# Three of the four up products of each MLP by a seven-product block scheme

## The reference

```python
def sq_relu_mlp(h, w_up, w_down):
    u = jnp.einsum('btd,df->btf', h, w_up)
    return jnp.einsum('btf,fd->btd', jnp.square(jax.nn.relu(u)), w_down)

h = h + sq_relu_mlp(rms_norm_2(h, mlp_norm_g[layer]), mlp_w_up[layer], mlp_w_down[layer])
```

## Time and profile before

| what | value |
|---|---|
| median of 3 runs | 1849.39 us (1848.42 to 1850.87) |
| the profiled execution | 1848.76 us |
| its span in the trace | 1847.0 us |
| TensorE busy (matmuls) | 1804.7 us, 98% |
| weight loads busy | 1441.0 us, 78% |
| VectorE busy | 981.4 us, 53% |
| ScalarE busy | 797.4 us, 43% |
| GpSimd busy | 476.5 us, 26% |
| DMA | 149.10 MB, 81 GB/s |

### The profile page before, as it was taken

How to read it: one execution, slowest core, us unless ns; L and a number is a source line. 1 busy time by engine, 2 the same in 40 slices (tenths; PEclk the granted TensorE clock), 3 DMA queues, 4 the chain that set the end, 5 groups by cost and what they waited for, 6 DMA issues and landing times.

```text
span 1847.0 us, 24633 instructions
## 1 busy us (share of the span) xinstructions
PE 1804.7 (98%) x9664; PEld 1441.0 (78%) x9668; DVE 981.4 (53%) x1581; ACT 797.4 (43%) x1401; POOL 476.5 (26%) x475
## 2 busy tenths in 40 slices
PE   7999999999999999999999999999999999999997
PEld 6987777776678766677888888888888788888886
DVE  5355556575546688854433434365677653333333
ACT  5236665455435365564441423233445543232412
POOL 0035551101312145560120201005677112010200
PEclk9999999999999999999999999999999999999999
DMA  5221111231012311012222222222222122222222
GB/s 182 93 71 54 48 46 60 82 97 48 23 57 96 124 65 34 30 36 70 91 102 103 92 92 102 103 91 81 81 86 75 57 92 100 96 97 97 95 98 79
DMA packets 44514, 149.10 MB, mean 81 GB/s; under 512 B 6000, under 2 KB 6384, under 8 KB 44400
## 3 DMA queue, kind: packets, MB, share of 16 engines
q1 hardware_dynamic: 44400, 147.53, 23.6%
HBM read 139.64 MB, written 2.10 MB: 77 GB/s over the span
## 4 chain that ended last, share of the span: by engine, by line
PE 87%; DVE 5%; POOL 3%; ACT 3%; issue 2%; DMA 1%; POOLq 0%; SPq 0%; DVEq 0%; ACTq 0%
PE BANK L288 23%; PE BANK L290 22%; PE BANK L289 22%; PE BANK L920 3%; PE BANK L654 2%; PE BANK L1704 1%; PE BANK L1685 1%; PE BANK L1661 1%; PE BANK L977 1%; PE BANK L2499 1%; PE BANK L639 1%; PE BANK L2474 1%; DVE LH L763 1%; POOL LH L885 1%; PE BANK L2462 1%
## 5 line engine op out<-in xcount | busy, mean ns | idle before, releaser
L256 ACT ACTIVATE WH<-WRAW 128x1024 fp32r<-128x1024 f32 x262 | 273.3, 1045 | 452.0 <-PE BANK L290 425.6
L265 DVE TENSOR_TENSOR WL<-WRAW,WH 128x1024 fp32r<-128x1024 f32 (+1 forms) x249 | 326.6, 1312 | 253.1 <-ACT WH L256 252.2
L288 PE MATMUL BANK<-HH,WH 128*128 128x512 f32 x1048 | 422.4, 403 | 11.1 <-DVE WL L265 9.6
L290 PE MATMUL BANK<-HL,WH 128*128 128x512 f32 x1048 | 409.4, 391 | 0.0
L289 PE MATMUL BANK<-HH,WL 128*128 128x512 f32 x1048 | 408.9, 390 | 0.0
L288 PEld LDWEIGHTS BANK<-HH,WH 128*128 128x128 f32 x1048 | 197.4, 188 | 60.5 <-issue 20.6
L290 PEld LDWEIGHTS BANK<-HL,WH 128*128 128x128 f32 x1048 | 197.1, 188 | 42.0
L289 PEld LDWEIGHTS BANK<-HH,WL 128*128 128x128 f32 x1048 | 197.6, 189 | 40.4 <-issue 2.9
L2339 POOL TENSOR_TENSOR HID<-TMP,HID 128x512 fp32r<-128x512 f32 x64 | 82.8, 1293 | 527.1 <-ACT HID L2320 527.1
L288 PE MATMUL BANK<-HID,WH 128*128 128x512 f32 (+1 forms) x520 | 200.8, 386 | 0.0
L290 PE MATMUL BANK<-HID,WH 128*128 128x512 f32 (+1 forms) x520 | 200.6, 386 | 0.0
(11 more groups left out here) (413 smaller groups left out, 3113.6 us busy)
## 6 DMA issues: line engine op xcount, KB each, us to landing
WRAW<-in_w SPq DMA_DIRECT2D x77, 512.0 KB, 3.4
WRAW<-in_wu SPq DMA_DIRECT2D x64, 512.0 KB, 3.2
WRAW<-in_wd SPq DMA_DIRECT2D x64, 512.0 KB, 3.2
WRAW<-in_w0o SPq DMA_DIRECT2D x8, 512.0 KB, 3.5
WRAW<-in_w1o SPq DMA_DIRECT2D x8, 512.0 KB, 3.4
WRAW<-in_wc SPq DMA_DIRECT2D x8, 512.0 KB, 3.2
WRAW<-in_w2o SPq DMA_DIRECT2D x8, 512.0 KB, 3.2
WRAW<-in_w3o SPq DMA_DIRECT2D x8, 512.0 KB, 3.2
```

Of the source, the lines that this page charges most:

```text
L256: e.activation(WH[b % NS][:, 0:n], WRAW[b % NR][:, 0:n], ACT.Copy).then_inc(*inc("s_high", ("high", b)))
L265: e.tensor_tensor(WL[b % NS][:, 0:n], WRAW[b % NR][:, 0:n], WH[b % NS][:, 0:n].bitcast(F32), ALU.subtract).then_inc(*inc("s_low_pool" if p ...
L288: e.matmul(dst, ah, bh, start=first and i == 0, stop=False)
L290: made = e.matmul(dst, ah, bl, start=False, stop=last and i == len(sets) - 1)
```

## The change

Chunk 0 of each MLP keeps its tiles. For chunks 1, 2 and 3 the up product is computed by Strassen's scheme in Winograd's form: the product of a 2 x 2 block matrix by another with seven block products instead of eight. The blocks are: output tiles m and m + 4 (a "pair", 0 to 3), planes k and k + 4 of the contraction, and the two halves of 256 tokens. The seven products use sums of weight blocks and sums of activation blocks as operands.

- **`fast_load`, `fast_sums`, `fast_high`, `fast_low`** replace load and split for the 24 blocks (`FAST`: chunk, pair, half of the contraction) of these up products. A block is again [128 x 1024], four quarters of 256; VectorE makes four sums of them (4 instructions of 256 elements), ScalarE copies the high parts of seven operands (1792 elements), VectorE subtracts for the low parts (1792 elements). `RAW` and `G` have three buffers.
- **`stage_vec`, `plane_mix`, `plane_high`, `plane_low`** make the activation operands once per MLP, while chunk 0's up tiles run: VectorE writes x times gain times `RS` (8 instructions of 512), GpSimd makes the sums (4 times 512, 256 and 256 elements), ScalarE and VectorE the high and low parts (4 times 1792 each). `RS` is so already in the operands.
- **`fast_pe`** issues for each of the 8 slots of a chunk 7 products x 2 planes x 3 matmuls of 256 columns. A pair (two slots) holds four fixed banks, 0 to 3 for even pairs, 4 to 7 for odd ones.
- **`first_act`, `join_first`, `join_last`** add the seven products to the four output blocks: one copy by ScalarE of 256, and on VectorE three instructions of 512 elements and one of 256 per pair. **`relu_act`** does relu, square and high part on ScalarE (3 of 1024 per pair), **`hid_low`** the low part on VectorE (1024 per pair). GpSimd has nothing in these chunks.
- **The order** becomes up 0, down 0, fast 1, down 1, fast 2, down 2, fast 3, down 3. Only one chunk is alive, so there is one pair of hidden buffers. The first two down tiles of each chunk first run over six planes each, then over the last two.
- Buffers move: the new ones lie over existing ones, `SCR` and `TMP` serve as `RAW`, and `ST`, `TRI`, `EHH`, `EHL` stand at other addresses.

The diff, cut to its core:

```diff
+FAST = [(c, pair, half) for c in range(1, 4) for pair in range(4) for half in range(2)]
...
         h_free = {"l1": ("tile", "l0k", 7), "mix0": ("tile", "m_g", 7), "mlp0": ("tile", "e", 14),
-                  "mix1": ("tile", ("up", 0, 3), 7), "mlp1": ("tile", ("o_v", 3), 3)}
+                  "mix1": ("fast used", 0, 23), "mlp1": ("tile", ("o_v", 3), 3)}
...
+        PRODUCTS = {"P1": (0, 6, 0, 0), "P2": (1, 4, 1, 0), "P6": (5, 2, 1, 1), "P7": (4, 0, 2, 0), "P5": (3, 1, 2, 1),
+                    "P4": (2, 3, 3, 0), "P3": (6, 5, 3, 1)}
+        ORDER = ("P1", "P2", "P6", "P7", "P5", "P3", "P4")
...
+        def fast_load(e, w, L, s):
+            if s > 2:
+                w.wait_ge(*at("fast low", L, s - 3))
+            else:
+                w.wait_ge(*at("hid lo", L, 0, 7))
+            e.dma_start(raw_part(s, 0, 4), A[f"wf{L}"][s]).then_inc(*dma(f"s_raw{s % 3}"))
...
+        def fast_high(e, w, L, s):
+            w.wait_ge(*at("sums", L, s))
+            if s > 2:
+                w.wait_ge(*at("fast used", L, s - 3))
+            else:
+                w.wait_ge(*at("plane low", L, 3))
...
+        def fast_pe(e, w, L, s):
+            c, pair, half = FAST[s]
+            if half == 0:
+                for j in range(4):
+                    _, was = banks.hold(("fast", L, c, pair, j), 4 * (pair % 2) + j,
+                                        ("first copied", L, c, pair) if j == 0 else ("joined", L, c, pair, (0, 1, 4, 3)[j]))
+                    for key in was:
+                        w.wait_ge(*at(*key))
+            w.wait_ge(*at("fast low", L, s))
+            wh, wl = G[s % 3][:, 0:7, :], G[s % 3][:, 7:14, :]
+            started = set()
+            for name in ORDER:
+                a, b, j, side = PRODUCTS[name]
+                dst = half_bank(pair, j, side)
+                for i in range(2):
+                    p = 2 * half + i
+                    w.wait_ge(*at("plane low", L, p))
+                    hi, lo = HP[p][:, b, :], HP[p][:, 7 + b, :]
+                    cols = slice(128 * i, 128 * i + 128)
+                    e.matmul(dst, wh[:, a, cols], hi, start=half == 0 and j not in started, stop=False, skip_group_check=True)
+                    started.add(j)
+                    e.matmul(dst, wl[:, a, cols], hi, start=False, stop=False, skip_group_check=True)
+                    made = e.matmul(dst, wh[:, a, cols], lo, start=False, stop=half == 1 and i == 1, skip_group_check=True)
...
         def mlp_tensor(e, w, L):
...
             for c in range(4):
+                if c:
+                    for s in range(8 * c - 8, 8 * c):
+                        fast_pe(e, w, L, s)
+                ks = (0, 4, 1, 5, 2, 6, 3, 7) if c else tuple(range(8))
+                for m in range(2):
+                    down(c, m, ks[0:6])
+                for m in range(2):
+                    down(c, m, ks[6:8])
+                for m in range(2, 7 if L and c == 3 else 8):
+                    down(c, m, ks)
...
         def mlp_vector(e, w, L):
...
+                if c:
+                    for i in range(9):
+                        s = first - 8 + i
+                        if i and not i % 2:
+                            join_last(e, w, L, c, i // 2 - 1)
+                        if 0 < i < 6:
+                            fast_low(e, w, L, s + 2)
+                        if i < 5:
+                            fast_sums(e, w, L, s + 3)
+                        if i > 5:
+                            split_low(e, w, block[("dn", L, c), i - 6], False)
+                        if i and not i % 2:
+                            hid_low(e, w, L, c, i // 2 - 1)
+                        if i % 2:
+                            join_first(e, w, L, c, i // 2)
...
                 for m in range(8):
                     add_x(e, w, ("dn", L, c), m)
+                    if m < 5:
                         split_low(e, w, after_block(("dn", L, c), m), False)
+                    if m > 4:
+                        fast_low(e, w, L, first + m - 5)
+                    if 3 < m < 7:
+                        fast_sums(e, w, L, first + m - 4)
...
         def mlp_scalar(e, w, L):
...
+                        if 0 < i < 6:
+                            fast_high(e, w, L, s + 2)
+                        if i > 5:
+                            split_high(e, w, block[("dn", L, c), i - 6])
+                        if i and not i % 2:
+                            relu_act(e, w, L, c, i // 2 - 1)
+                        if i % 2:
+                            first_act(e, w, L, c, i // 2)
...
     def mlp(layer):
...
+        out = first
         for c in range(4):
+            if c:
+                out += fast[8 * c - 5:8 * c]
+            out += down[8 * c:8 * c + 8]
             if c < 3:
+                out += fast[8 * c:8 * c + 3]
```

More of the change, by code:

```diff
@@ new lines, in join_last, with relu_act @@
+        def join_last(e, w, L, c, pair):
+            key = (L, c, pair)
+            w.wait_ge(*at("product", *key, "P4"))
+            e.tensor_tensor(Q[:, 0:4:3, :], Q[:, 5:7, :], pair_bank(pair, 3), ALU.add).then_inc(
+                *inc("s_joined", ("joined", *key, 3)))
+        def relu_act(e, w, L, c, p):
+            q = flat(Q[:, 0:4, :])
+            w.wait_ge(*at("joined", L, c, p, 3))
+            e.activation(q, q, ACT.Relu).then_inc(*inc("s_relu", ("relu", L, c, p)))
+            w.wait_ge(*at("relu", L, c, p))
+            e.activation(q, q, ACT.Square).then_inc(*inc("s_relu", ("fast square", L, c, p)))
+            w.wait_ge(*at("fast square", L, c, p))
+            e.activation(flat(HIDH[:, 4 * p:4 * p + 4, :]), q, ACT.Copy).then_inc(*inc("s_hid", ("hid hi", L, c, p)))
@@ L2296, in mlp_vector @@
[L2296 to L2302, removed]
+            for m in range(8):
+                if m == 0:
+                    factor_vec(e, w, g)
+                w.wait_ge(*at("tile", ("up", L, 0), m))
+                if m > 3:
+                    w.wait_ge(*at("hid lo", L, 0, m - 4))
+                e.scalar_tensor_tensor(out=TMP[:, m % 4, :], in0=banks[("up", L, 0), m], scalar=0.0, in1=RS[:, :],
+                                       op0=ALU.max, op1=ALU.mult).then_inc(*inc("s_evac", ("evac", ("up", L, 0), m)))
+                split_low(e, w, after_block(("up", L, 0), m), False)
+                if m < 4:
+                    stage_vec(e, w, L, m)
+                if m in (3, 4):
+                    plane_low(e, w, L, m - 3)
@@ new lines, in mlp_vector @@
+            for p in (2, 3):
+                plane_low(e, w, L, p)
+            for c in range(4):
+                first = 8 * c
+                if c:
[13 more added lines that the diff above has]
+                            join_first(e, w, L, c, i // 2)
+                if c == 3:
+                    break
+                for m in range(8):
+                    add_x(e, w, ("dn", L, c), m)
+                    if m < 5:
@@ new lines, in mlp_scalar @@
+            for p in (2, 3):
+                plane_high(e, w, L, p)
+            for c in range(4):
+                first = 8 * c
+                if c:
+                    for i in range(9):
+                        s = first - 8 + i
+                        if 0 < i < 6:
[6 more added lines that the diff above has]
+                            first_act(e, w, L, c, i // 2)
+                if c == 3:
+                    break
+                for m in range(8):
+                    if m < 5:
@@ L2328, in mlp_scalar @@
                         split_high(e, w, after_block(("dn", L, c), m))
+                    if m > 4:
+                        fast_high(e, w, L, first + m - 5)
             if L == 0:
@@ L3035, in sync @@
             o_swaps = {block[o_slots[s]] + NS + NR: s for s in o_swapped}
-            for b in range(NR, len(stream)):
+            for _, _, _, key in plan[NR:]:
+                if key[0] == "fast":
+                    fast_load(e, w, *key[1:])
+                    continue
+                b = block[key]
                 for pair in m_swaps.get(b, ()):
```

218 lines of the change are left out of this document (152 added, 66 removed).

## The result

The changed kernel takes 1852.40 us (median; 1850.99 to 1859.66), the kernel before 1849.56 on the same chips: ratio 1.0019, 95% interval 1.0011 to 1.0026. It is a little slower, where 12.4 us less were forecast. The prediction was wrong.

What follows compares the result with a forecast made beforehand. TensorE, without idle time in the MLPs, was taken as the bound; 19.2 us saved less 6.8 at the banks gave 12.4 us less, 1837.0 from the median of 1849.39; forecast 1834 to 1840 (chance 0.67), range 1830 to 1846.

Steps and rivals of the forecast that it cites:

- TensorE's saving: Up products of both MLPs: 576 full-width products removed, 1008 half-width added at 0.120 us; 9.6 us per MLP, 19.2 both.
- The stop at the banks: At each fast stage's start TensorE waits for the addition of down tile 7: 1.13 us, six times, 6.8 us.
- The fast stages: VectorE and ScalarE in chunks 1 to 3 fall behind and catch up; least low-part margin 2.8 us, no TensorE stop.
- The last handover: End of each fast stage: pair 3's low part ready at 48.3 us, needed by the down product at 48.5; fits by 0.2.
- (a): Fast stages: pair 3's low part late, TensorE stops 0.5 to 1.3 us each, 3 to 8 us back, 1840 to 1845; chance 0.15.
- (b): Fast stages: VectorE becomes the bound, kernel slower; 1869 if its instructions take 17% more; chance 0.09.
- The first chunk: Chunk 0's up stage: VectorE's added work sums to 29.4 of 43.5 us, so no TensorE stop, cost 0.
- one step of 6.5 us hides: Chunk 0's up stage: weights are split three tiles ahead, so one VectorE step of 6.5 us wouldn't stop TensorE.
- rival (d): Clock falls to the lower level behind each of six bank stops, 2.1 us lost each, 12.7 us: 1849.7, no change; chance 0.03.

Runs made afterwards that it cites:

- the own banks: Against the changed kernel, down tile m takes bank m instead of the next of the ring: 1844.53 us, ratio 0.9970.

## Why the prediction was wrong

**TensorE's saving: right.** 0.120 us per half-width product was forecast. The timeline of TensorE in the changed kernel's fast stage has (986.41 - 984.73)/14 = 0.120:

```profile
...
984.73 0.28 PE L2383 MATMUL BANK<-HP,G 128*128 128x256 f32 x1
...
986.41 0.28 PE L2382 MATMUL BANK<-HP,G 128*128 128x256 f32 x1
```

19.2 us were forecast for both MLPs; with no stop left it is 9.53 + 9.55 = 19.1. The weight loads (0.192 us each now) overlap. Of the two prices the rows' was the right one, not the estimated 28.5 by the isolated formula of the Trainium skill (TensorE: Matmul & The Clock Gate, Back-to-back issue gap).

**The stop at the banks: right in place and number, a little too small.** Six waits, on bank 3, for the addition to X. Forecast 1.13 each, 1.2 to 1.3 in the trace, and taking them away gave 1.28 each in the first MLP; the term that was too small is the time from the addition's end to TensorE's next product, 0.26 to 0.36 for 0.15.

**The fast stages: right.** The working had the low parts 4 to 7 end at 15.3, 20.8, 27.1 and 32.5 us from the start of slot 0; from 975.78 in the trace they end at 15.0, 20.3, 26.1 and 31.4. VectorE's timeline of the changed kernel has the last of them (L2327) and hid_low of pair 3 (L2429):

```profile
...
1005.10 2.03 DVE L2327 TENSOR_TENSOR G<-RAW,G 128x1792 fp32r<-128x1792 f32 x1 [0.62 <-ACT G L2322]
...
1020.99 1.23 DVE L2429 TENSOR_TENSOR HIDL<-Q,HIDH 128x1024 fp32r<-128x1024 f32 x1 [2.17 <-ACT HIDH L2425]
```

The down product starts at 975.78 + 40.3 = 1016.1 and needs pair 3 at 1024.3; the low part ends at 1022.2. The last handover had 0.2 us to spare in the working and has 2.1 in the trace, in the main since independent VectorE instructions overlap by 0.08 us, as the prediction said but didn't use; it put that at a little more than 1 us, and how the rest divides was not taken apart. fast_low takes 2.02 for the 2.03 taken. Rivals (a) and (b) didn't happen; the run with four more additions shows that (b) was a real danger. Where it begins is only bracketed: 1.7 us more on the chain to pair 3 cost nothing, 5.7 us cost 8 us per stage.

**The first chunk: wrong.** "Cost 0" is the step that failed; for the two MLPs together the runs show 14.0 us in its place. It added up VectorE's work, 29.4 of 43.5 us, and took the rest as room. But VectorE works in order, and 2.31 us of each tile it stands idle behind ScalarE, with an instruction at its head that can't start. This time was in the trace of before, in the same instructions; this is VectorE's timeline there, in the kernel before:

```profile
...
894.17 0.68 DVE L2293 SCALAR_TENSOR_TENSOR TMP<-BANK,RS 128x512 f32<-128x512 f32 x1
897.16 1.48 DVE L265 TENSOR_TENSOR WL<-WRAW,WH 128x1024 fp32r<-128x1024 f32 x1 [2.31 <-ACT WH L256]
898.56 0.68 DVE L2293 SCALAR_TENSOR_TENSOR TMP<-BANK,RS 128x512 f32<-128x512 f32 x1
```

The split began 2.31 us after the evacuation's end, and the step was 4.39 us (894.17 to 898.56) even where VectorE was behind and hurried, so the room was about 1 us per tile. stage_vec needs 1.4 us of it alone and 2.45 beside GpSimd, whose slowing the prediction applied to the splits only. 0.69 + 2.31 + 1.23 + 2.44, less what overlaps, is the 6.50 us that the trace shows, over 5.44, and "one step of 6.5 us hides" held for one step, where there were five in a row over 5.44 (5.7, 6.5, 6.5, 8.4 and 7.0), behind a VectorE that starts late each time because of the norm's factor. The trace of before would have warned even without any slowing of stage_vec: eight steps of 4.39 us, four times 1.4 for stage_vec and twice 2.03 for the two plane_low ahead of the last split are an estimated 44.8 us for a stage of 43.5. The price in the first MLP: 349.73 - 3 x 1.28 = 345.89, against 339.53, is 6.4 us. In the second it is 340.28 - 3 x 1.28 = 336.44, against 328.84: 7.6, of which 1.3 is the longer stretch at the low clock.

**The clock: rival (d) in another place.** It was tied to the stops of 1.1 us, and behind those the clock stayed at 1.00. Behind the stops of 3.7 us, which the prediction didn't have, it fell: 1.6 us lost in the first MLP, 2.9 in the second.

The sum as measured: the saving is 19.1, and the MLPs take 2.6 more than before, so 21.7 us were given back: 7.7 at the banks (6 x 1.28) and the other 14.0 in the first chunks, 4.5 of them by the clock. The forecast gave back 6.8, all of it at the banks.

## What to carry to other kernels

Room on an engine that works in order is not its idle time. Write down one period of it with its waits: what stands at the head of its queue, who releases it, and what an added instruction pushes back; new work belongs into a wait, ahead of the instruction that waits, and 2.4 us moved by one place were worth 12 us here. Add the waits to the sum of the work before calling the rest room, and price a new instruction beside the engines that will run next to it. And look at the stages that a change only burdens as closely as at those that it speeds up.

## What the runs showed that was not expected

- A stop of TensorE costs more than its length when it is long: behind 3.7 us of idle time seven products of 512 columns in one MLP and thirteen in the other came about 0.43 us or more apart instead of 0.227; behind 1.1 us the granted clock stayed at 1.00. With the own banks it was seven in both. Why thirteen once is open.
- Beside GpSimd's instructions two scalar_tensor_tensor of 512 elements on VectorE took 2.3 to 3.6 us instead of 1.4, and GpSimd's low part of 512 elements took 2.32 beside them instead of 1.29: the slowing goes both ways. GpSimd's timeline in the changed kernel's first chunk:

```profile
...
893.60 1.30 POOL L2555 TENSOR_TENSOR HIDL<-TMP,HIDH 128x512 fp32r<-128x512 f32 x1 [55.70 <-ACT HIDH L2523]
...
900.27 2.32 POOL L2555 TENSOR_TENSOR HIDL<-TMP,HIDH 128x512 fp32r<-128x512 f32 x1
```

- TensorE needed 0.26 to 0.36 us from the end of the addition that it waited for to its next product of 256 columns, where the one stop in the trace of before had shown 0.15, with 512 columns. What makes the difference was not tried.
